# Recurrence of a two-block model on one core: level 1's products sent ahead of the state sums on TensorE, and VectorE's order moved to match

## What is computed

```python
def hgrn2_scan(q, k, v, log_f, s0, with_outputs):
    """Chunkwise S_t = diag(f_t) S_{t-1} + k_t v_t^T, o_t = S_t^T q_t along axis 2."""
    ...
o_f, oc_f = hgrn2_direction(q, i, zf, lb_f, qc, ic, zfc, ctx_out, reverse=False)
o_b, oc_b = hgrn2_direction(q, i, zb, lb_b, qc, ic, zbc, ctx_out, reverse=True)
y = hgrn2_readout(o_f + o_b, g, g_norm, w_out)
```

## Time and profile before

| | |
|---|---|
| Runs | 2344.57, 2348.21, 2349.40 us; median 2348.21 |
| Profiled execution | 2346.51 us, its span 2344.5 us |
| Granted PE clock, mean | 0.970 |
| Busy: PE, DVE, ACT, POOL | 92%, 45%, 29%, 35% of the span |
| Recurrence | about 567 to 1042 us of the span |

### The profile page before, as it was taken

The page is one execution under the profiler, slowest core; times in us unless marked ns, Lnnn a source line. Parts: engine busy times, 40 slices in busy tenths (PEclk is TensorE's granted clock), DMA queues, the critical chain, the costliest instruction groups (busy, mean ns, idle before and its releaser), DMA issues. The chain is left out here.

```text
span 2344.5 us, 27285 instructions
## 1 busy us (share of the span) xinstructions
PE 2151.1 (92%) x11287; PEld 1717.0 (73%) x11287; DVE 1063.8 (45%) x1685; ACT 668.5 (29%) x1043; POOL 810.5 (35%) x429
## 2 busy tenths in 40 slices
PE   4999888989898989987898899999998999999998
PEld 3887777866575757776855678888887688888886
DVE  2113664663555555557995543111126684111114
ACT  3223223334545454642112432100113353000111
POOL 1421113311333333325500015553544234554453
PEclk7999999999999999999899999999999999999999
DMA  9242113433111111113111112322322222232332
GB/s 300 72 116 74 55 55 91 126 109 90 36 36 36 36 36 37 36 55 99 41 36 54 55 54 72 105 93 91 107 90 90 83 97 72 90 108 90 93 96 81
DMA packets 183114, 187.41 MB, mean 80 GB/s; under 512 B 25728, under 2 KB 162256, under 8 KB 182864
## 3 DMA queue, kind: packets, MB, share of 16 engines
q1 hardware_dynamic: 173040, 175.42, 24.4%
q10 hardware_dynamic: 9376, 8.16, 1.3%
q0 software_dynamic: 576, 2.10, 0.2%
HBM read 183.56 MB, written 2.10 MB: 79 GB/s over the span
## 5 line engine op out<-in xcount | busy, mean ns | idle before, releaser
L3011 POOL TENSOR_TENSOR weights_lo<-weights_raw,weights_hi 128x2048 fp32r<-128x2048 f32 (+1 forms) x101 | 457.6, 4531 | 865.5 <-ACT weights_hi L1429 669.4
L698 PE MATMUL ring<-input_hi,weights_hi 128*128 128x512 f32 x784 | 305.4, 390 | 4.1 <-POOL weights_lo L3011 4.1
L700 PE MATMUL ring<-input_hi,weights_lo 128*128 128x512 f32 x784 | 305.0, 389 | 0.0
L699 PE MATMUL ring<-input_lo,weights_hi 128*128 128x512 f32 x784 | 305.0, 389 | 0.0
L2837 DVE CAST weights_hi<-weights_raw 128x2048 fp32r<-128x2048 f32 (+1 forms) x72 | 87.7, 1218 | 366.2 <-PE ring L700 173.9
L2998 POOL TENSOR_TENSOR h_w<-h_p 128x512 f32<-128x512 f32 x56 | 73.6, 1314 | 381.9 <-PE ring L1013 265.1
L989 PE MATMUL obank<-acts,weights_raw 128*128 128x512 f32 x384 | 179.6, 622 | 0.0
L698 PEld LDWEIGHTS ring<-input_hi,weights_hi 128*128 128x128 f32 x784 | 147.2, 188 | 36.4 <-issue 5.9
L700 PEld LDWEIGHTS ring<-input_hi,weights_lo 128*128 128x128 f32 x784 | 147.2, 188 | 30.5
L699 PEld LDWEIGHTS ring<-input_lo,weights_hi 128*128 128x128 f32 x784 | 147.2, 188 | 30.4
L998 PE MATMUL obank<-weights_raw,acts 128*128 128x256 f32 x640 | 142.7, 380 | 0.0
(11 more groups left out here) (465 smaller groups left out, 4429.2 us busy)
## 6 DMA issues: line engine op xcount, KB each, us to landing
weights_raw<-in_w_ada SPq DMA_DIRECT2D x24, 1024.0 KB, 5.4
weights_raw<-in_ffn_w_gate SPq DMA_DIRECT2D x22, 1024.0 KB, 5.4
weights_raw<-in_ffn_w_up SPq DMA_DIRECT2D x22, 1024.0 KB, 5.4
weights_raw<-in_ffn_w_down SPq DMA_DIRECT2D x16, 1024.0 KB, 5.0
weights_raw<-in_w_in_c SPq DMA_DIRECT2D x12, 1024.0 KB, 5.2
weights_raw<-in_w_in_ab SPq DMA_DIRECT2D x9, 1024.0 KB, 7.2
weights_raw<-in_w_in_c SPq DMA_DIRECT2D x16, 512.0 KB, 5.3
weights_raw<-in_ev_w_in SPq DMA_DIRECT2D x8, 1024.0 KB, 5.5
```

What stands on the lines that cost most here:

```text
L698: pe.matmul(o, hi[:, k, ms], xh[:, k, t0:t0 + n], start=k == 0, stop=False)
L699: pe.matmul(o, hi[:, k, ms], xl[:, k, t0:t0 + n], start=False, stop=False)
L700: last = pe.matmul(o, lo[:, k, ms], xh[:, k, t0:t0 + n], start=False, stop=k == KD - 1)
L3011: pool.tensor_tensor(W_LO[slot][:, 0:kt, :], WR[:, slot, 0:kt, :], w_hi[:, 0:kt, :], ALU.subtract).then_inc(sem("w_lo"), 1)
```

## The change

On PE, level 1's products move from behind the diagonal to a place ahead of the state products. On DVE, level 2's operand moves from behind the diagonal to a place ahead of the last head's outputs, and level 1's copy from behind the diagonal to a place behind those outputs.

```diff
@@ -1089,6 +1089,7 @@
                 between(0)
                 if st:
                     inside(st - 1, True)
+                levels(st, 1)
                 pe.wait_ge(*product_emptied(("i", hb, 2)))
                 for part, js in enumerate((range(0, 4), range(4, 5))):
                     pe.wait_ge(*read_of(f"kt{st}.{part}"))
@@ -1106,7 +1107,6 @@
                     cs = slice(c * P, (c + 1) * P)
                     last = pe.matmul(ps[:, cs], HKS[:, cs], Q_[:, hj, cs], start=True, stop=True)
                 last.then_inc(filled, 1)
-                levels(st, 1)
                 between(1)
                 levels(st, 2)
                 between(2)
@@ -2414,13 +2414,13 @@
                 level_operand(7 * st + 1)
                 keys_of_both(st)
                 level_scores(st, 0)
+                level_operand(7 * st + 2)
                 if st:
                     inside(st - 1, True)
+                level_scores(st, 1)
                 query_operand(st)
                 states(st)
                 diagonal(st)
-                level_operand(7 * st + 2)
-                level_scores(st, 1)
                 level_operand(7 * st + 3)
                 level_scores(st, 2)
                 if st == LAST:
```

## The result

The changed kernel takes 2314.2 us (median of 4 runs, 2313.4 to 2318.0) against 2346.4 us for the kernel before in the same series (2344.3 to 2349.4). The ratio is 0.9865, 95% interval 0.9848 to 0.9882: 32 us less, between 28 and 36. A repeat beside the experiments gave 0.9881 (0.9864 to 0.9897). The forecast was 2319.5 us, 28.7 less than before, inside its range of 2312 to 2331.

What follows compares the result with a forecast made beforehand. TensorE (PE), busy 92% of the span, was taken to bound the kernel, with time won only where it waits or runs slowed. Gains of 20.8 + 7.9 = 28.7 us gave 2319.5 us, range 2312 to 2331.

Steps and rivals of the forecast that it cites:

- What bounds, and the bank: PE bounds; before level 1 it waits for a PSUM bank that DVE reads late: 8 waits, 20.9 us.
- Term 1: PE's waits before level 1 go: 2.80 us in seven steps, 1.2 to 1.3 in step 0, 20.8 us in all.
- The new wait: On PE before the diagonal, for DVE's copy of level 1: 0.07 us in each of seven steps.
- Term 2: Five stretches of product work at the lowered clock behind PE's wait go: 7.9 us, with 0 as other end.
- Level 5's waits: PE's waits before level 5 in steps 0, 2 and 4, and the slowed work behind, stay: nothing counted.
- The operand's move, cost 0: On DVE, level 2's operand ahead of the last head's outputs: cost 0, cover 3 us or more.
- Rival 1: PE's stretches at the lowered clock stay or turn up elsewhere: 2327.4 us; chance 0.13.
- all later stages take as long as before: Sign of being right: stages behind the recurrence keep their length, the recurrence being 27 to 30 us shorter.
- Rival 2: POOL holds DVE's square for one instruction of 1.09 us, and the diagonal with it: 7.6 less gained, 2327.1; chance 0.10.
- Rival 3: POOL holds all three DVE instructions ahead of the diagonal: PE waits 3.37 us there, 2353.7 us in all; chance 0.02.
- Rival 4: PE's 18 waits on level operands (L2305) grow by what PE comes earlier: 2340 to 2348 us; chance 0.05.

Runs made afterwards that it cites:

- four squares: The changed kernel with DVE's square of the last head's outputs made five times instead of once in seven steps: 2360.5 us, ratio 1.0065.
- one more square: The changed kernel with DVE's square of the last head's outputs made twice instead of once in seven steps: 2326.7 us, ratio 0.9926.
- two more: The changed kernel with DVE's square of the last head's outputs made three times instead of once in seven steps: 2339.5 us, ratio 0.9980.

## Why the prediction was right

- **What bounds, and the bank.** Right, and shown by the two half edits: level 1's move alone brings the gain, the operand alone nothing.
- **Term 1, 20.8 us.** It measured 21.5 (29.4 less 7.9 of clock). The new wait was taken as 0.07 us in seven steps and is 0.11 to 0.14 in six, the gain of a step without the clock as 2.80 and is 2.82 (steps 3 and 5). Step 0 gave 1.4, not 1.2. Step 6, with the longest wait before (3.01 us) and no new one, gave 3.2 without its clock, 0.4 more than the others.
- **Term 2, 7.9 us.** The five slowed stretches are gone, and their excess over step 3 in the kernel before is 7.9 us. That they follow from the wait was an assumption then. The squares show it: put the wait back, and they come back.
- **Level 5's waits, counted at nothing.** 3.31 us as before, slowed as before (713.66, 715.53 above), in three of three steps. From level 4 to level 6 the three steps take 2.0 us more than in the kernel before, since more of the work is slowed; the waits before level 0 in steps 1, 3 and 5 are 2.0 us less (1.8 where they were 3.9). The two cancel. A likely reason, not tested by itself, is that level 0 of the next step waits for a chain that the slowed products don't lengthen. The prediction saw neither, so its nothing came out right without its reason.
- **The operand's move, cost 0.** Right; it brings nothing either.
- **Rival 1 (slowed stretches stay)** did not come inside the recurrence. Something like it came outside: the output projection began slow in the changed kernel, 2.0 us, and so it did in four more of the eleven profiles (1.5 to 1.9 us). The prediction's sign that all later stages take as long as before did not hold in this profile (4.0 us more).
- **Rival 2 (POOL holds the square)** is real and was seen, once in the run with level 1's move alone (1.0 us), and in all seven steps of the runs with more squares. In the changed kernel DVE was ahead by 0.21 us, which I had put at 0.14; with that little the order turned once in another run, so the margin was thin.
- **Rival 3 (slower)** did not come, but the four squares are its picture: 4.3 us of new wait make the kernel slower than before.
- **Rival 4 (given back)**: the waits on L2305 went down, not up.
- The median lies 5.3 us below the forecast. 0.7 us is term 1. The rest isn't assigned: 1.8 is the median of before, 2346.4 with a fourth run where the prediction had 2348.2, and the remainder is no more than the spread of the runs and of the parts outside the recurrence.

## What to carry to other kernels

When an engine waits for the reader of a buffer in a ring, look at which unit it waits for, and change the order of takes so that the unit that waits follows one whose reader comes early, and long work stands ahead of the take that needs the late reader's bank. Here that order was worth 29.4 us of the recurrence, and the waiting engine's own instructions stayed the same. Price such a wait with the clock behind it: here 20.9 us of waits cost another 7.9. And size a new wait with the neighbour that takes turns with the reader's engine: four more squares on DVE delayed the diagonal by 4.3 us where their own time is 2.9, with POOL at work beside them.

## What the runs showed of the hardware

Slowed stretches against the length of PE's wait before them, counted in these profiles: none of 7 at 1.3 to 1.5 us (one more square), 4 of 7 at 2.4 to 2.5 (two more), 5 of 7 at 2.6 to 2.7 (operand alone) and 5 of 7 at 2.8 to 3.0 (before), all 27 at 3.31 in nine profiles, all 7 at 4.1 to 4.3 (four more squares), all 6 at 4.6 to 4.7 (the two runs with projection work moved). A wait of 1.97 us before level 0 in step 0 had one in one of eleven profiles (level 1 alone). I hadn't expected so gradual a growth: between 2.4 and 3.0 us equal waits had it in one step and not in the next. With seven cases a run the shares in between are rough, and the work ahead of the wait isn't the same in all of them. The Trainium skill (TensorE: Matmul & The Clock Gate, What's actually happening) has the gate judge recent activity in periods that run freely of the kernel; steps 1 and 2 of the run with two more squares, with equal waits and different clocks, agree.

A DVE instruction with both inputs in SBUF and a POOL instruction took turns in the rows above: the one that came second grew longer, L2367 1.43 instead of 0.69 us in one case, POOL's L2998 1.43 instead of 1.09 in the other, five squares 5.01 instead of 3.65. The copy from PSUM (L2326) and the reduction (L2368) kept 0.73 and 0.69 us beside POOL. The Trainium skill (SBUF — State Buffer, Who interferes with whom) says that a DVE instruction with two inputs in SBUF contends with a GpSimd instruction that reads SBUF, and one with at most one such input doesn't. Both halves are seen here.
